# Stick-breaking sums from two rounded parts, and the heads in pairs

## The reference, cut to what matters

```
z       = q . k / 8                       # queries t by keys s, per head
mask    = s < t                           # strictly causal
log_1m  = where(mask, log_sigmoid(-z), 0)
rev     = reverse cumulative sum of log_1m over s
log_w   = log_sigmoid(z) + (rev - log_1m)
w       = where(mask, exp(log_w), 0)
out     = w . v
```

## Time and profile before

| | us |
|---|---|
| median of the runs | 1362.68 |
| the profiled execution, whole | 1362.74 |
| its span, first to last instruction | 1361.0 |
| PE busy in the span | 1319.0 |
| VectorE / ScalarE / GpSimd busy | 916.1 / 667.0 / 31.2 |
| mean granted TensorE clock, share of full speed | 0.995 |

### The profile page before, as it was taken

The page is one execution under the profiler, slowest core; times in us unless marked ns, Lnnn a source line. Parts: engine busy times, 40 slices in busy tenths (PEclk is TensorE's granted clock), DMA queues, the critical chain, the costliest instruction groups (busy, mean ns, idle before and its releaser), DMA issues.

```text
span 1361.0 us, 21812 instructions
## 1 busy us (share of the span) xinstructions
PE 1319.0 (97%) x8766; PEld 1185.1 (87%) x8766; DVE 916.1 (67%) x1091; ACT 667.0 (49%) x764; POOL 31.2 (2%) x52
## 2 busy tenths in 40 slices
PE   7999999999999999998999999999999999999997
PEld 7998888888977888887998989999989988999997
DVE  4647666566455766558566787777686758877775
ACT  5635444435464544445454644444555445544454
POOL 0000000000021000001000000000020000000000
PEclk9999999999999999999999999999999999999999
DMA  9634655554523555553543345555545424555520
GB/s 369 243 125 155 247 185 186 185 186 159 184 91 124 187 188 192 193 195 118 174 153 108 141 167 182 185 183 184 179 152 183 139 87 160 186 185 185 185 93 32
DMA packets 33490, 229.85 MB, mean 169 GB/s; under 512 B 3728, under 2 KB 3984, under 8 KB 6032
## 3 DMA queue, kind: packets, MB, share of 16 engines
q1 hardware_dynamic: 31536, 220.21, 46.1%
q10 hardware_dynamic: 1888, 8.68, 1.8%
HBM read 227.83 MB, written 1.05 MB: 168 GB/s over the span
## 4 chain that ended last, share of the span: by engine, by line
PE 85%; DVE 7%; ACT 4%; issue 2%; DMA 1%; SPq 0%; POOL 0%; DVEq 0%; ACTq 0%
PE ring L336 18%; PE ring L334 9%; PE ring L277 9%; PE ring L278 8%; PE ring L279 8%; PE acc L379 4%; PE acc L381 4%; PE acc L380 4%; PE acc L277 3%; PE acc L279 3%; PE acc L278 3%; DVE wlo L269 2%; ACT whi L261 2%; PE ring L379 1%; PE ring L380 1%
## 5 line engine op out<-in xcount | busy, mean ns | idle before, releaser
L269 DVE TENSOR_TENSOR wlo<-raw,whi 128x2048 fp32r<-128x2048 f32 x207 | 475.1, 2299 | 183.2 <-ACT whi L261 183.0
L261 ACT CAST whi<-raw 128x2048 fp32r<-128x2048 f32 x207 | 393.9, 1907 | 109.4 <-PE ring L279 48.5
L336 PE MATMUL ring<-xs,whi 128*128 128x512 f32 x1184 | 420.0, 398 | 0.0
L334 PE MATMUL ring<-xs,wlo 128*128 128x256 f32 x1184 | 333.2, 281 | 0.2
L336 PEld LDWEIGHTS ring<-xs,whi 128*128 128x128 f32 x1184 | 222.5, 188 | 53.4
L277 PE MATMUL ring<-xs,whi 128*128 128x256 f32 x832 | 242.2, 291 | 13.3 <-DVE wlo L1544 6.4
L278 PE MATMUL ring<-xs,whi 128*128 128x256 f32 x832 | 236.6, 284 | 0.0
L279 PE MATMUL ring<-xs,wlo 128*128 128x256 f32 x832 | 236.5, 284 | 0.0
L334 PEld LDWEIGHTS ring<-xs,wlo 128*128 128x128 f32 x1184 | 223.8, 189 | 2.1 <-DVE wlo L269 1.0
L277 PEld LDWEIGHTS ring<-xs,whi 128*128 128x128 f32 x832 | 160.7, 193 | 18.5 <-issue 7.4
L278 PEld LDWEIGHTS ring<-xs,whi 128*128 128x128 f32 x832 | 160.9, 193 | 1.1 <-issue 1.0
(11 more groups left out here) (267 smaller groups left out, 1723.5 us busy)
## 6 DMA issues: line engine op xcount, KB each, us to landing
raw<-wstream SPq DMA_DIRECT2D x207, 1024.0 KB, 4.9
sq<-lnp ACTq DMA_DIRECT2D x4, 1024.0 KB, 4.9
cst<-consts ACTq DMA_DIRECT2D x1, 1029.0 KB, 14.8
hT<-xT SPq DMA_DIRECT2D x4, 256.0 KB, 4.9
raw<-wstream SPq DMA_DIRECT2D x4, 256.0 KB, 5.9
hT<-xtok ACTq DMA_DIRECT2D x1, 1024.0 KB, 18.8
misc<-decay ACTq DMA_DIRECT2D x1, 1024.0 KB, 4.8
out<-y SPq DMA_DIRECT2D x4, 256.0 KB, 2.3
```

Of the source, the lines that this page charges most:

```text
L261: act.copy(whi[:, c % SPLIT, :], raw[:, c % RAW, :]).then_inc(hi_made, 1)
L269: dve.tensor_tensor(wlo[:, c % SPLIT, :], raw[:, c % RAW, :], whi[:, c % SPLIT, :].bitcast(f32), ALU.subtract).then_inc(lo_made, 1)
L334: pe.matmul(bank(b + t)[:, 0:256], wl[:, w], xhi[:, k, :], start=k == 0, stop=False, skip_group_check=True)
L336: mm = pe.matmul(bank(b + t), wh[:, w], xs[:, k, :, :].rearrange("p a s -> p (a s)"), start=False, stop=k == NT - 1, skip_group_check=True)
```

## The change

The softplus terms are split into two float32r parts, and the sums are made from these with float32r copies of the two sign matrices. The masked `yf` is rounded by GpSimd into a slot of `hhi`, right behind the mask. VectorE subtracts that part from `yf` into a slot of `hlo`. PE then runs four matmuls per head in place of two: `tri_r` with the high and the low part (384 columns each), `neg_r` with both (128 columns each). The sign matrices are copied once, by GpSimd.

GpSimd's order becomes softplus mask, rounding, weight mask of head h-2. VectorE's order becomes, for each pair p: low parts of pair p, softplus of pair p+1, abs of pair p+2. ScalarE's becomes logs of pair p+1, then both weights of pair p. On PE, sums of head 2 no longer stand ahead of the scores of pair 2; from pair 1 on one loop holds the order sums, scores, values, sums. The wait for the sums of four heads ago moves from the softplus to the two parts.

```diff
+        signs = sb("signs", [128, 256], f32r)
+        tri_r, neg_r = signs[:, 0:128], signs[:, 128:256]
+        def sp_part(t, h):
+            return t[:, :, :, :].rearrange("p a b s -> p (a b s)")[:, (h % 4) * 384:(h % 4) * 384 + 384]
...
             def sb_sums(h):
-                b, L = sb_bank(h), yf[:, (h % 4) * 384:(h % 4) * 384 + 384]
+                b = sb_bank(h)
+                high, low = (sp_part(t, h) for t in (hhi, hlo))
+                if h == 0:
+                    pe.wait_ge(signs_made, 1)
                 pe.wait_ge(s_L, h + 1)
-                pe.matmul(b[:, 0:384], tri, L, start=False, stop=False, skip_group_check=True)
-                pe.matmul(b[:, 128:256], neg, L[:, 256:384], start=False, stop=True,
+                for part in (high, low):
+                    pe.matmul(b[:, 0:384], tri_r, part, start=False, stop=False, skip_group_check=True)
+                pe.matmul(b[:, 128:256], neg_r, high[:, 256:384], start=False, stop=False, skip_group_check=True)
+                pe.matmul(b[:, 128:256], neg_r, low[:, 256:384], start=False, stop=True,
                           skip_group_check=True).then_inc(s_lw, 1)
...
-            sb_sums(2)
             sb_scores(2)
-            sb_sums(3)
-            sb_scores(3)
-            sb_values(0)
-            for p in range(2, SB_H // 2):
+            for p in range(1, SB_H // 2):
                 sb_sums(2 * p)
                 if p + 2 < SB_H // 2:
                     sb_scores(p + 2)
...
-            for h in range(4, SB_H):
-                sb_weights(h - 2)
-                sb_logs(h)
-                if h in (9, 13, 15):
-                    sb_out_high((9, 13, 15).index(h))
-            sb_weights(SB_H - 2)
-            sb_weights(SB_H - 1)
+            for p in range(1, SB_H // 2):
+                if p + 1 < SB_H // 2:
+                    sb_logs(2 * p + 2)
+                    sb_logs(2 * p + 3)
+                sb_weights(2 * p)
+                sb_weights(2 * p + 1)
+                if p in (3, 5, 7):
+                    sb_out_high((3, 5, 7).index(p))
...
+            def sb_low(h):
+                s = (h % 4) * 384
+                dve.wait_ge(s_hi, h + 1)
                 if h >= 4:
                     dve.wait_ge(s_lw, h - 3)
-                dve.scalar_tensor_tensor(yf[:, s:s + 384], sb_bank(h)[:, 0:384], 0.0, a, ALU.max, ALU.add).then_inc(s_sp, 1)
+                dve.tensor_tensor(sp_part(hlo, h), yf[:, s:s + 384], sp_part(hhi, h).bitcast(f32), ALU.subtract).then_inc(s_L, 1)
...
             ahead(C_SB_IN, 10)
-            for h in (0, 1):
-                sb_abs(h)
-            for h in (0, 1):
-                sb_softplus(h)
+            both(sb_abs, 0)
+            both(sb_softplus, 0)
             split_lo(dve, C_SB_IN + 10 + AHEAD)
-            for h in (2, 3):
-                sb_abs(h)
-            for h in (2, 3):
-                sb_softplus(h)
+            both(sb_low, 0)
+            both(sb_abs, 2)
+            both(sb_softplus, 2)
             split_lo(dve, C_SB_IN + 11 + AHEAD)
-            sb_abs(4)
-            sb_abs(5)
-            sb_softplus(4)
-            sb_abs(6)
-            sb_abs(7)
-            sb_softplus(5)
-            sb_abs(8)
-            sb_abs(9)
-            for p in range(3, SB_H // 2):
-                sb_softplus(2 * p)
-                sb_softplus(2 * p + 1)
+            both(sb_abs, 4)
+            for p in range(1, SB_H // 2):
+                both(sb_low, 2 * p)
+                if p + 1 < SB_H // 2:
+                    both(sb_softplus, 2 * p + 2)
                 if p + 2 < SB_H // 2:
-                    sb_abs(2 * p + 4)
-                    sb_abs(2 * p + 5)
+                    both(sb_abs, 2 * p + 4)
...
+            pool.wait_ge(const_in, 16)
+            pool.tensor_copy(signs[:, :], cst[:, CONST["tri"]:CONST["tri"] + 256]).then_inc(signs_made, 1)
             for h in range(SB_H + 2):
+                if h < SB_H:
+                    pool.wait_ge(s_sp, h + 1)
+                    own.sync(strict(yf[:, (h % 4) * 384:(h % 4) * 384 + 384]))
+                    if h >= 4:
+                        pool.wait_ge(s_lw, h - 3)
+                    pool.tensor_copy(sp_part(hhi, h), yf[:, (h % 4) * 384:(h % 4) * 384 + 384]).then_inc(s_hi, 1)
                 if h >= 2:
                     g = h - 2
                     pool.wait_ge(s_w, g + 1)
                     strict(sqf[:, (g % 4) * 384:(g % 4) * 384 + 384]).then_inc(s_wm, 1)
-                if h < SB_H:
-                    pool.wait_ge(s_sp, h + 1)
-                    strict(yf[:, (h % 4) * 384:(h % 4) * 384 + 384]).then_inc(s_L, 1)
```

More of the change, by code:

```diff
@@ L171, in build_program @@
              "ktd", "ktc", "ud", "st", "od", "sq", "var", "rs"))
-        s_z, s_abs, s_ln, s_sp, s_L, s_lw, s_w, s_wm, s_o = (sem("sb_" + n) for n in ("z", "abs", "ln", "sp", "L", "lw", "w", "wm", "o"))
+        signs_made = sem("signs_made")
+        s_z, s_abs, s_ln, s_sp, s_hi, s_L, s_lw, s_w, s_wm, s_o = (sem("sb_" + n) for n in ("z", "abs", "ln", "sp", "hi", "L", "lw", "w", "wm", "o"))
         wf_in = sem("wf_in")
@@ L1635, in sb_softplus, with both @@
                 dve.wait_ge(s_ln, h + 1)
+                dve.scalar_tensor_tensor(yf[:, s:s + 384], sb_bank(h)[:, 0:384], 0.0, a, ALU.max, ALU.add).then_inc(s_sp, 1)
+            def sb_low(h):
+                s = (h % 4) * 384
+                dve.wait_ge(s_hi, h + 1)
                 if h >= 4:
                     dve.wait_ge(s_lw, h - 3)
-                dve.scalar_tensor_tensor(yf[:, s:s + 384], sb_bank(h)[:, 0:384], 0.0, a, ALU.max, ALU.add).then_inc(s_sp, 1)
+                dve.tensor_tensor(sp_part(hlo, h), yf[:, s:s + 384], sp_part(hhi, h).bitcast(f32), ALU.subtract).then_inc(s_L, 1)
             def sb_out_low(j):
                 x_low(4, lambda i: pair(acc, i % 2), [j])
+            def both(f, h):
+                f(h)
+                f(h + 1)
             ahead(C_SB_IN, 10)
-            for h in (0, 1):
-                sb_abs(h)
-            for h in (0, 1):
-                sb_softplus(h)
+            both(sb_abs, 0)
+            both(sb_softplus, 0)
             split_lo(dve, C_SB_IN + 10 + AHEAD)
-            for h in (2, 3):
-                sb_abs(h)
-            for h in (2, 3):
-                sb_softplus(h)
+            both(sb_low, 0)
+            both(sb_abs, 2)
+            both(sb_softplus, 2)
             split_lo(dve, C_SB_IN + 11 + AHEAD)
-            sb_abs(4)
-            sb_abs(5)
-            sb_softplus(4)
-            sb_abs(6)
-            sb_abs(7)
-            sb_softplus(5)
-            sb_abs(8)
-            sb_abs(9)
-            for p in range(3, SB_H // 2):
-                sb_softplus(2 * p)
-                sb_softplus(2 * p + 1)
+            both(sb_abs, 4)
[3 more added lines that the diff above has]
+                    both(sb_softplus, 2 * p + 2)
                 if p + 2 < SB_H // 2:
-                    sb_abs(2 * p + 4)
-                    sb_abs(2 * p + 5)
+                    both(sb_abs, 2 * p + 4)
                 if p in (4, 6, 7):
```

## The result

The changed kernel takes 1369.97 us in the median (1369.4 to 1370.9), against 1362.39 us for the kernel before in the same runs: a ratio of 1.0056, with a 95% interval from 1.0043 to 1.0068. It is slower by 7.6 us, outside the predicted range (1360.8 to 1368.2) and clear of the forecast "no change". The profiled execution took 1369.71 us, its span 1367.9.

What follows compares the result with a forecast made beforehand. A loop of waits through all engines was taken to bound the stage, none being full. The walked steps gave +0.6 us and three SBUF port meetings +1.2, so +1.8 on 1362.74: 1364.5 us, range 1360.8 to 1368.2.

Steps and rivals of the forecast that it cites:

- no change: Whole kernel: time within 0.3%, 4.1 us, of the kernel before, given a chance of 0.81.
- the clock falls: Rival, PE in the stage: idle stretches bring half clock, +3.5 to +5 us, 1366 to 1368; chance 0.06.
- Its longest pause: PE in the stage: longest idle stretch foreseen, 390.8 to 392.4, given as 1.8 us.
- Copy: GpSimd's rounding of the masked `yf`, 128x384 from float32 to float32r: taken as 0.48 us.
- Low part to sums: From VectorE's low part to PE's start of the sums: 0.60 us, bounds 0.47 and 1.2.
- The start of head 2's sums: Start of the stage on PE: at 392.4, 3.5 us after the old start, projection ending near 389.0.
- The blocks at the SBUF: VectorE's low parts meeting GpSimd at the shared read port: three places on the path, 0.4 each, 1.2 us.
- The walk without them: Steps added through the stage without port blocks: last sums end at 418.3 against 417.65, +0.6 us.
- A head's sums: Four float32r matmuls on PE: held for about 0.60 us a head in place of 1.06.
- GpSimd did not become the bound: Rival, GpSimd in the stage: bound from copy 0.41 with every block paid, 0.78 with none; up to +7.8 us; chance 0.18.
- PE was the bound: Rival, the stage follows PE's busy time: 6.4 us off less 1.8 lost, -4.6 us, 1358.1; chance 0.04.
- a loss at the start: Start of the stage: 1.8 us lost on PE, with scores of pair 2 ahead of head 2's sums.

Runs made afterwards that it cites:

- fill2: Changed kernel plus idle matmuls into free banks, in PE's pauses ahead of the sums of heads 2, 6, 10 and 14; 1363.44 us, ratio 1.0004 to the kernel before.
- fill2_port: fill2 with the low part made as zero from PSUM, so that VectorE needs nothing of SBUF for it; 1364.05 us, ratio 1.0009 to the kernel before.
- chain_long: Changed kernel with its order, rounding, low parts and waits, but sums from `yf` by two float32 matmuls; 1369.61 us, ratio 1.0049 to the kernel before.
- best0: Kernel before without the split, with an order of heads written out for each engine; 1358.98 us, ratio 0.9970 to the kernel before.
- fill_first: fill2 with only its first group of idle matmuls, 3 ahead of the sums of head 2; 1368.74 us, ratio 1.0040 to the kernel before.
- best1: Changed kernel's split with an order of heads written out for each engine; 1360.41 us, ratio 0.9982 to the kernel before.

## Why the prediction was wrong

**The step that failed is the rival "the clock falls".** The prediction reasoned from one row, an idle stretch of 3.22 us with the clock at 0.50 behind it, that pauses of at most 1.8 us would leave the clock alone, and gave this 0.06; the sum itself has no term for the clock. Its longest pause was a slip as well: 390.8 to 392.4 is 1.6 us, not 1.8, and its own steps hold longer ones. Head 9's sums, 7.54 us behind head 5's at 398.1, end at 406.2, and head 10's start at 408.6: a pause of about 2.3 us (measured: 2.23). The runs show falls of the clock around pauses of 1.57, 1.66, 1.82, 1.91, 1.95, 2.06, 2.23, 2.24 and 2.60 us. One row of a long pause shows that a fall can follow it, not that less is safe. It also priced the case at one or two stretches of 3.5 us and up to 1368; there were three, the first of 6.8 us, and 1370.

**What the clock cost.** Stage 34.4 against 30.2 us in fill2: 4.2. The output projection began at the low clock: from its start to the load of the next gains on ScalarE's queue 30.5 us (423.09 to 453.57) against 29.3 (419.17 to 448.43): 1.2. The last 1.6 of the 6.8 us between these two spans come later: near 801 and near 1160 the changed kernel ran at the low level for 3.4 us each, as the kernel before did, and fill2 did not (below).

**Most steps held.** Copy: 0.50 for 0.48. Low part to sums: 0.60 (401.54 to 402.14), as taken, and 0.74 where it met GpSimd (419.79 to 420.53). Pause ahead of head 2: 1.57 for "near 1.7". The start of head 2's sums 3.3 us after the projection's end, walked 3.4. Stage at full clock: +1.7 for +1.8.

**Terms that were off and cancelled.** That the stage came out at +1.7 is in part luck. The blocks at the SBUF cost 0.3, not 1.2. The walk without them said +0.6, and fill2_port, which has none, stands at +1.4. A head's sums hold PE for 0.72 (start steps of 0.28, 0.18, 0.06 and 0.20), not 0.60; with some four of them on the walk's path that is about 0.5 us, an estimate. Part of the rest may be the run's own idle matmuls, that delay head 6's sums a little. That was not separated. The bottom of the range has a slip too: 1362.4 less 1.8 is 1360.6, not 1360.8.

**The other rivals.** GpSimd did not become the bound: the copy is 0.50, over the 0.41 at which it was to decide with every block paid, but the blocks cost 0.3 in all, and without them the point is 0.78. "PE was the bound" is refuted by fill2: at full clock the stage is 1.7 us longer than before, where this rival has it 4.6 shorter. chain_long can't settle it, since its clock fell less often as well. The parts of the change were never weighed against each other in the prediction: the order gains 2.4 us where I had put it down as a loss at the start, and the split costs about 10 with that order, its low clock included.

## What to carry to other kernels

Where PE waits in a loop, work taken off PE may turn into a lower clock: price it with the pauses that it leaves, and let no row of a long pause stand for a safe length. Look at the granted clock by stretch before explaining a longer stage by its waits; a few idle matmuls in the pauses, into a bank that is free at that point, tell the two apart in one run. And split a change of order from a change of arithmetic: here the order was the gain (best0, 4.1 us by its ratio with no split at all).

## What the runs showed of the hardware that I had not expected

**The clock goes with the spread.** Behind pauses of equal length, 1.57 us, the clock fell in one execution and not in two others. The same goes on outside the stage. In the second stack PE has a pause of 3.2 us near 790 us, and another near 1150; these stretches ran at 0.83 in the kernel before (first two rows) and at 1.00 in fill2 (last three), although its pause was as long. There fill2, 1.7 us behind at the stage's end, drew level by the end of the span:

```profile
790.00:800.00 10.00, 6.78 (x43) 6.47 (x42) 8.23 (x11) 5.41 (x6) 0.00 (x0) 0.83 0.30 106
1150.00:1160.00 10.00, 7.25 (x48) 7.25 (x49) 8.97 (x12) 5.43 (x6) 0.00 (x0) 0.83 0.29 105
```

```profile
795.33 0.39 PE L285 MATMUL acc<-hhi,whi 128*128 128x256 f32 x1 [3.21 <-DVE wlo L277]
...
790.00:800.00 10.00, 6.79 (x52) 6.27 (x51) 7.49 (x12) 4.98 (x5) 0.00 (x0) 1.00 0.31 106
1150.00:1160.00 10.00, 6.49 (x51) 5.97 (x49) 8.25 (x11) 5.42 (x6) 0.00 (x0) 1.00 0.31 107
```

Even the kernel before ranges from 1360.72 us at a mean clock of 0.997 to 1364.8 at 0.994. What decides whether a given pause counts was not settled. In the stage, the clock fell around each pause over 1.9 us in the profiled executions of the changed kernel, fill_first and chain_long, and around none of those under 1.5 us in best1's; but fill2's two of 3.21 us in the second stack left it at 1.00, so length alone does not decide.
